# Key-index sums and the rotary of the latent heads on GpSimd instead of VectorE, in a two-block transformer kernel

## The chip, the cores and the metric

One core of a Trainium2 chip. The metric is the device time of one execution in microseconds (us), the median of several runs. All data is float32.

## What is computed

The reference runs a first block of two layers over 256 tokens of width 1024 and then a second block. Each of the two layers modulates and normalises x, projects it (`w_in`), runs four kinds of attention side by side (four heads of 64 each), projects back, and goes on to a feed-forward part (dense in layer 0, eight experts in layer 1). The four kinds are A (differential), B (latent), C (indexed sparse) and D (banded). The change touches two pieces of them:

```
# B, latent attention: rotary on the last 32 of each query head's 96 values and on the shared key part
q = concatenate([q[..., :64], apply_rope(q[..., 64:], cos, sin)])
k_rope = apply_rope(kr, cos, sin)
k = concatenate([k_nope, broadcast(k_rope)])
# apply_rope: [x1*cos - x2*sin, x1*sin + x2*cos], halves of 16

# C, indexed sparse attention: a score for each key, summed over eight index heads with weights
score = relu(einsum('bqhd,bsd->bqhs', qib, k_idx))
score = einsum('bqhs,bqh->bqs', score, wb)
score = where(mask, score, -inf)
top_val, top_idx = top_k(score, 64)
```

Only the 64 chosen keys take part in C's softmax.

## The kernel before, in words

The kernel is one program with a stream of instructions for each engine, written out by hand in order; semaphores are the only link between engines, and nothing is reordered. SyncE streams the weights in chunks of 1 MB into a ring of six; ScalarE and VectorE split each piece into a high and a low part (L1118 and L1688), and TensorE makes three products of each (L565 to L567). In the attention no weights are split, until its end.

The 256 tokens are two blocks of 128 rows (b = 0, 1) on the partitions. A unit of attention, such as A10, is a kind, a block b and a part; block 0 sees 128 keys, block 1 sees 256. For A the parts are the two terms of the difference, for I (the key index of C) they are index heads 0 to 3 and 4 to 7. A unit goes through:

- TensorE's `score` (L769): four heads into PSUM. TensorE waits for the result of the unit two places before.
- VectorE's `bias` (L1866 to L1869): scale and bias table added in PSUM, then the negative maximum of each head. Units I have none.
- ScalarE's `probabilities`: exponentials (L1292), or for I a ReLU (L1287), from PSUM into `PR`, a tile with two places (`place(...) % 2`) of four heads of up to 256 keys. Before it writes, ScalarE waits until the unit two places before has been used. For A10 that is I00's sum, for A11 I01's sum, for B00 I10's sum and for B10 I11's sum (semaphore `idx_added`); for I10 it is the turn of A11.
- TensorE's `turn` (L783) and ScalarE's `copy_pT` (L1302), TensorE's `values` (L798), VectorE's `store` (L1923).

The order of scores is A00 A01 I00 I01 A10 A11 I10 I11 B00 B10 D00 D10 C00 C10. VectorE's order is in its `attention`, printed below. There:

- `index_add` (L1883): `total = src * weight + total`, four instructions in a row for a unit's four heads, each waiting for the one before; the first takes the mask `cmask` (part 0) or the sum so far (part 1). The total lies in `picks[b]`. `w16` (weights) comes from `prepare_index` (semaphore `c_ready`).
- `select_keys` (L1894 to L1896): eight rounds of MAX8 and MATCH_REPLACE8 on the total, for block 0 after `combine` of A11, for block 1 after the store of B00.
- `rope_latent`: when ScalarE has copied B4 and B5, the up-projected keys and values (`copy_latent_out`, L1262), it makes the rotary of the four query heads and of the shared key part (L1952 to L1957) for both blocks, and copies the keys into `KB` (L1967, L1968). TensorE's fills B6 to B9 (L698) wait for it (`b_roped`), and ScalarE copies each out of PSUM (L1270). In TensorE's order: fill B6, fill B7, score I11, fill B8, turn A11, fill B9, fill D0, scores B00 and B10.
- `combine` (L1903 to L1909) makes the difference of A's two terms in place.
- `store_squares` and `store_normed` normalise A's output. Between them GpSimd raises four sums to the power -0.5 (`root`, L451; asked with L1623, taken with `take_root`).

In the attention GpSimd has one memset (`KI4`) and three such powers, in the order `root(0, 4)`, `root(4, 8)`, `root(4, 8)`. Outside it GpSimd issues the loads of the modulation weights `ada` (L438), each behind VectorE's use of an earlier one (`ada_used`), and some tables. SyncE's ring loads wait for VectorE's low parts of the weights.

## Time and profile before

| what | value |
|---|---|
| median of 3 runs | 2196.5 us (2195.31 to 2198.93) |
| the profiled execution's own time | 2199.03 us |
| its span, first to last instruction | 2197.3 us |
| mean granted TensorE clock | 0.963 |
| attention of layer 0 and of layer 1 (TensorE's first fill to its first product after it) | 120.5 to 201.4 us, 506.0 to 586.5 us |

How to read it: L12 is line 12 of the kernel. PE is TensorE's products, PEld its weight loads, DVE VectorE, ACT ScalarE, POOL GpSimd, SP SyncE. A timeline row has the start in us from the span's start, the duration in us (of all `xN` instructions together), engine, line, operation, output and inputs with partitions x elements, and in brackets the idle time of the engine ahead of it with what ended it. `arena` holds `PR` and the projections, `xt_words` the sums, `KB` and small tiles, `ps` is PSUM. Waits are inferred from semaphore events.

### The profile page before, as it was taken

The page shows a single profiled execution, that of the slowest core. Times are in us where ns is not written, and L with a number is a line of the kernel's source. Part 1 is how long each engine was busy: PE and PEld are TensorE (multiplying, and loading weights), DVE is VectorE, ACT ScalarE, POOL GpSimd, SP SyncE. Part 2 cuts the span into 40 slices and gives each one's busy share as a digit, 9 for nine tenths or more (in the row PEclk, how much of TensorE's full clock was granted, in tenths as well). Part 3 has the DMA queues.
Part 4 walks back from the last instruction along what each step waited for, and adds up shares of the span by engine and source line. Part 5 has one row for each costly group of instructions (what it writes and reads, how often), then busy time and mean ns, then how long its engine had stood idle before and what let it go on. Part 6 is the DMA issues. An engine that isn't in the chain of part 4 may idle for free.

```text
span 2197.3 us, 26426 instructions
## 1 busy us (share of the span) xinstructions
PE 2058.7 (94%) x9646; PEld 1699.0 (77%) x9646; DVE 1674.2 (76%) x2026; ACT 1333.9 (61%) x1834; POOL 55.6 (3%) x92
## 2 busy tenths in 40 slices
PE   3978999997899999999999999999979999889998
PEld 2757788885778888888888888888858887777887
DVE  5777677786668999989898999989986555345554
ACT  1444344444448878888887878888864445464443
POOL 1000000000000000000000000000000000000000
PEclk8987999998799999999999999999989999989999
DMA  8922587671159989999998989999965554304551
GB/s 348 367 103 88 195 333 295 262 300 50 60 231 351 375 336 374 362 347 363 347 368 345 373 338 373 363 347 364 374 233 195 188 192 153 134 20 156 190 191 58
DMA packets 80615, 573.67 MB, mean 261 GB/s; under 512 B 9088, under 2 KB 9728, under 8 KB 12272
## 3 DMA queue, kind: packets, MB, share of 16 engines
q1 hardware_dynamic: 70112, 508.59, 60.8%
q0 software_dynamic: 7936, 57.05, 6.7%
q10 hardware_dynamic: 2448, 6.41, 0.8%
q8 instruction: 78, 1.28, 0.2%
q14 instruction: 41, 0.34, 0.0%
HBM read 570.97 MB, written 1.05 MB: 260 GB/s over the span
## 4 chain that ended last, share of the span: by engine, by line
PE 85%; DVE 8%; ACT 3%; DMA 2%; issue 1%; POOL 1%; ACTq 0%; DVEq 0%; POOLq 0%
PE ps L565 25%; PE ps L567 25%; PE ps L566 25%; DMA Z<-in_ada 1%; PE ps L964 1%; PE ps L516 1%; PE ps L937 1%; PE ps L769 1%; PE ps L798 1%; DMA arena<-in_ada 1%; ACT arena L1292 1%; PE ps L783 1%; DVE Z L1593 1%; PE ps L629 1%; DVE xt_words L1895 1%
## 5 line engine op out<-in xcount | busy, mean ns | idle before, releaser
L2144 DVE TENSOR_TENSOR weights_low<-ring,weights_high 128x1024 fp32r<-128x1024 f32 x668 | 797.3, 1222 | 47.6 <-ACT weights_high L1396 34.9
L1396 ACT ACTIVATE weights_high<-ring 128x1024 fp32r<-128x1024 f32 x668 | 706.7, 1060 | 92.2 <-PE ps L567 79.2
L565 PE MATMUL ps<-weights_high,xt_high 128*128 128x512 f32 x1832 | 735.0, 401 | 13.1 <-DVE xt_low L1664 5.2
L567 PE MATMUL ps<-weights_high,xt_low 128*128 128x512 f32 x1832 | 719.1, 393 | 0.0
L566 PE MATMUL ps<-weights_low,xt_high 128*128 128x512 f32 x1832 | 718.6, 392 | 0.0
L1118 ACT ACTIVATE weights_high<-ring 128x1024 fp32r<-128x1024 f32 x298 | 313.7, 1058 | 309.7 <-PE ps L567 294.6
L1688 DVE TENSOR_TENSOR weights_low<-ring,weights_high 128x1024 fp32r<-128x1024 f32 x298 | 362.2, 1223 | 177.2 <-ACT weights_high L1118 176.8
L565 PEld LDWEIGHTS ps<-weights_high,xt_high 128*128 128x128 f32 x1832 | 346.8, 189 | 84.0 <-DVE xt_low L1664 5.7
L567 PEld LDWEIGHTS ps<-weights_high,xt_low 128*128 128x128 f32 x1832 | 346.4, 189 | 74.1
L566 PEld LDWEIGHTS ps<-weights_low,xt_high 128*128 128x128 f32 x1832 | 347.5, 190 | 68.4 <-issue 0.8
L565 PE MATMUL ps<-weights_high,hT_high 128*128 128x512 f32 x688 | 268.5, 390 | 1.2 <-DVE hT_low L2154 1.2
L567 PE MATMUL ps<-weights_high,hT_low 128*128 128x512 f32 x688 | 267.7, 389 | 0.0
L566 PE MATMUL ps<-weights_low,hT_high 128*128 128x512 f32 x688 | 267.7, 389 | 0.0
L565 PEld LDWEIGHTS ps<-weights_high,hT_high 128*128 128x128 f32 x688 | 129.1, 188 | 28.5 <-DVE hT_low L2154 1.6
L566 PEld LDWEIGHTS ps<-weights_low,hT_high 128*128 128x128 f32 x688 | 129.2, 188 | 26.9 <-issue 0.2
L567 PEld LDWEIGHTS ps<-weights_high,hT_low 128*128 128x128 f32 x688 | 129.1, 188 | 26.9
L1405 ACT ACTIVATE hT_high<-ps 128x256 fp32r<-128x256 f32 x112 | 42.8, 382 | 49.5 <-PE ps L937 49.5
L451 POOL TENSOR_TENSOR rstd<-rstd,minus_half 128x1 f32<-128x1 f32 (+2 forms) x28 | 22.7, 811 | 1754.9 <-DVE rstd L1623 1754.8
L516 PE MATMUL ps<-xt_words,X 128*128 128x128 f32 x160 | 26.6, 340 | 42.9 <-DVE xt_words L1639 42.8
L2154 DVE TENSOR_TENSOR hT_low<-ps,hT_high 128x256 fp32r<-128x256 f32 x112 | 46.8, 418 | 22.9 <-ACT hT_high L1405 22.9
L1401 ACT ACTIVATE FS<-ps 128x256 f32<-128x256 f32 x112 | 43.0, 384 | 30.8 <-PE ps L567 30.8
L798 PEld LDWEIGHTS ps<-arena 128*128 128x128 f32 x320 | 50.2, 244 | 12.3 <-issue 6.8
(234 smaller groups left out, 1444.7 us busy)
## 6 DMA issues: line engine op xcount, KB each, us to landing
ring<-in_stream SPq DMA_DIRECT2D x483, 1024.0 KB, 4.9
Z<-in_ada POOLq DMA_DIRECT2D x42, 1024.0 KB, 5.9
arena<-in_ada POOLq DMA_DIRECT2D x6, 1024.0 KB, 16.7
Z<-in_na POOLq DMA_DIRECT2D x1, 2048.0 KB, 7.8
Z<-in_dil POOLq DMA_DIRECT2D x1, 2048.0 KB, 13.5
band<-in_band ACTq DMA_DIRECT2D x2, 768.0 KB, 19.6
X<-in_x SPq DMA_DIRECT2D x1, 1024.0 KB, 11.3
gate_mix<-in_rows ACTq DMA_DIRECT2D x2, 512.0 KB, 8.9
```

The source lines that it names most:

```text
L516: return nc.tensor.matmul(ps[:, kt // 2, (kt % 2) * T + b * P:(kt % 2) * T + (b + 1) * P], source[:, b, kt * P:(kt + 1) * P], diag, start= ...
L565: nc.tensor.matmul(out, xh, wh, start=n, stop=False, skip_group_check=True)
L566: nc.tensor.matmul(out, xh, wl, start=False, stop=False, skip_group_check=True)
L567: return nc.tensor.matmul(out, xl, wh, start=False, stop=last, skip_group_check=True)
L798: m = nc.tensor.matmul(ps[:, 6, h * HD:(h + 1) * HD], PT[:, h, kb, :], PROJ[:, kb, c:c + HD], start=kb == 0, stop=kb == u.nk // P - 1)
L1118: act.activation(WH[:, p % SPLITS, :], ring[:, chunk % RING, half * PIECE:(half + 1) * PIECE], ACT.Copy).then_inc(hi_ready, 1)
L1396: act.activation(WH[:, slot, :], raw, ACT.Copy).then_inc(m["hi_ready"], 1)
L1401: act.activation(sgt[:, par, :], ps[:, 4 + par, 0:FW], ACT.Silu).then_inc(m["silu_ready"], 1)
L1405: act.activation(hTH[:, par].rearrange("p f n -> p (f n)"), ps[:, 6 + par, 0:2 * P], ACT.Copy).then_inc(m["hT_hi"], 1)
L1688: nc.vector.tensor_tensor(WL[:, p % SPLITS, :], ring[:, chunk % RING, half * PIECE:(half + 1) * PIECE], WH[:, p % SPLITS, :].bitcast(F32), ...
L2144: nc.vector.tensor_tensor(WL[:, slot, :], raw, WH[:, slot, :].bitcast(F32), ALU.subtract).then_inc(m["lo_ready"], 1)
L2154: nc.vector.tensor_tensor(hTL[:, par].rearrange("p f n -> p (f n)"), ps[:, 6 + par, 0:2 * P], hTH[:, par].rearrange("p f n -> p (f n)").bi ...
```

## The change

VectorE's `index_add`, `rope` and `rope_latent` go, and GpSimd gets them. The rotary keeps its instructions. The index sum has another form: one multiplication of all four heads by their weights, in place in `PR`, one addition of two heads to two, one of one to one, and one to the mask or to the sum so far: four instructions where each waits for the one before by a new semaphore, `pool_turn` (`turned_by`). The semaphores that others wait for (`idx_added`, `b_roped`) are unchanged. GpSimd's three powers stand in one list with the new work, `attention_sums`. VectorE's order is else unchanged.

```diff
+            turns = [0]
+            def index_add(layer, name):
+                u = UNIT[name]
+                b, nk, number = u.b, u.nk, INDEXED(layer, name)
+                total = picks[b][:, 0, :]
+                pool.wait_ge(probs, WEIGHED(layer, name))
+                if u.part == 1:
+                    pool.wait_ge(idx_added, number - 1)
+                rows = PR[:, place(layer, name) % 2, :, 0:nk]
+                weights = w16[:, b, 4 * u.part:4 * u.part + 4]
+                at = 0 if b == 0 else 128
+                heads = rows.rearrange("p (a b) k -> p a b k", a=2)
+                slots = weights.rearrange("p (b a) -> p a b", b=2).unsqueeze(3).broadcast_to([P, 2, 2, nk])
+                turned_by(pool.tensor_tensor(heads, heads, slots, ALU.mult))
+                turned_by(pool.tensor_tensor(rows[:, 0:2, :], rows[:, 0:2, :], rows[:, 2:4, :], ALU.add))
+                turned_by(pool.tensor_tensor(rows[:, 0, :], rows[:, 0, :], rows[:, 1, :], ALU.add))
+                ins = pool.tensor_tensor(total, rows[:, 0, :], cmask[:, at:at + nk] if u.part == 0 else total, ALU.add)
+                ins.then_inc(idx_added, 1)
+            def rope(x, b):
...
+                pool.tensor_tensor(TR[:, 0, 0:n], x1, cos, ALU.mult)
+                pool.tensor_tensor(TR[:, 1, 0:n], x2, sin, ALU.mult)
+                pool.tensor_tensor(TR[:, 2, 0:n], x1, sin, ALU.mult)
+                turned_by(pool.tensor_tensor(TR[:, 3, 0:n], x2, cos, ALU.mult))
+                pool.tensor_tensor(x1, TR[:, 0, 0:n], TR[:, 1, 0:n], ALU.subtract)
+                turned_by(pool.tensor_tensor(x2, TR[:, 2, 0:n], TR[:, 3, 0:n], ALU.add))
+            def turned_by(ins):
+                turns[0] += 1
+                ins.then_inc(pool_turn, 1)
+                pool.wait_ge(pool_turn, turns[0])
+            def rope_latent(layer):
+                pool.wait_ge(filled, FILLED(layer, "B5"))
+                for b in range(NB):
+                    q = PROJ[:, b, B_UQ:B_UQ + 384].rearrange("p (h n) -> p h n", h=4)
+                    rope(q[:, :, 64:96], b)
+                    rope(PROJ[:, b, B_KR:B_KR + 32].unsqueeze(1), b)
+                    kv = PROJ[:, b, B_UKV:B_UKV + 512].rearrange("p (h n) -> p h n", h=4)
+                    pool.tensor_copy(KB[:, b, :, 0:64], kv[:, :, 0:64])
+                    ins = pool.tensor_copy(KB[:, b, :, 64:96],
+                                           PROJ[:, b, B_KR:B_KR + 32].unsqueeze(1).broadcast_to([P, 4, 32]))
+                ins.then_inc(b_roped, 1)
+            def attention_sums(layer):
+                root(0, 4)
+                pool.wait_ge(c_ready, layer + 1)
+                index_add(layer, "I00")
+                index_add(layer, "I01")
+                root(4, 8)
+                rope_latent(layer)
+                index_add(layer, "I10")
+                index_add(layer, "I11")
+                root(4, 8)
...
-            root(0, 4)
-            for b in range(NB):
-                root(4, 8)
+            attention_sums(0)
...
-            root(0, 4)
-            for b in range(NB):
-                root(4, 8)
+            attention_sums(1)
...
                 combine(layer, 0)
-                index_add(layer, "I00")
-                index_add(layer, "I01")
                 bias(layer, "A10")
                 store_squares(layer, "A01")
                 bias(layer, "A11")
-                rope_latent(layer)
                 combine(layer, 1)
                 select_keys(layer, 0)
-                index_add(layer, "I10")
                 store_normed(layer, "A01")
-                index_add(layer, "I11")
                 bias(layer, "B00")
```

## Rows read from the trace of the kernel before

**Rows 1.** The page's first part: busy time of each engine.

```profile
PE 2058.7 (94%) x9646; PEld 1699.0 (77%) x9646; DVE 1674.2 (76%) x2026; ACT 1333.9 (61%) x1834; POOL 55.6 (3%) x92
```

**Rows 2.** Windows view, two stretches of the first attention.

```profile
core 0: us, PE busy (x) PEld busy (x) DVE busy (x) ACT busy (x) POOL busy (x), PEclk, DMA share, GB/s
139.00:162.00 23.00, 15.91 (x84) 11.64 (x83) 21.66 (x78) 11.52 (x28) 1.01 (x1) 0.93 0.00 1
162.00:190.00 28.00, 22.32 (x133) 19.07 (x132) 24.78 (x54) 12.04 (x46) 1.01 (x1) 0.73 0.00 1
```

**Rows 3.** The chain that ended last: start us, us, what.

```profile
159.45 0.48 DVE xt_words L1883
...
168.59 2.09 PE ps L769 x8
...
170.71 1.24 DVE ps L1866
```

**Rows 4.** VectorE's timeline, first attention: start us, us, instruction, idle before.

```profile
136.43 2.74 DVE L1883 SCALAR_TENSOR_TENSOR xt_words<-arena,w,xt_words 128x128 f32<-128x128 f32 x7
...
145.54 0.21 DVE L1952 TENSOR_TENSOR xt_words<-arena,cossin 128x64 f32<-128x64 f32 x1
...
149.71 0.22 DVE L1968 COPY xt_words<-arena 128x128 f32<-128x128 f32 x1
...
158.41 1.53 DVE L1883 SCALAR_TENSOR_TENSOR xt_words<-arena,w,xt_words 128x256 f32<-128x256 f32 x3
...
160.65 2.04 DVE L1883 SCALAR_TENSOR_TENSOR xt_words<-arena,w,xt_words 128x256 f32<-128x256 f32 x4
```

**Rows 5.** Timeline of all engines, first attention, ahead of the rotary.

```profile
128.21 0.23 DVE L1623 TENSOR_SCALAR rstd<-ss 128x2 f32<-128x2 f32 x2
...
136.99 1.13 PE L769 MATMUL ps<-arena 32*128 32x256 f32 x8
...
141.89 0.47 ACT L1292 ACTIVATE arena<-ps,nmax 128x256 f32<-128x256 f32 x1
...
143.69 0.62 ACT L1262 ACTIVATE arena<-ps 128x512 f32<-128x512 f32 x1
```

**Rows 6.** GpSimd's timeline, up to the loads after the first attention.

```profile
5.71 0.12 POOL L461 MEMSET minus_half<- 128x8 f32 x1
...
117.69 0.95 POOL L470 MEMSET FS<- 128x1024 f32 x1 [0.34 <-DVE lamc L2284]
...
128.52 1.04 POOL L451 TENSOR_TENSOR rstd<-rstd,minus_half 128x4 f32<-128x4 f32 x1 [9.88 <-DVE rstd L1623]
...
213.35 0.59 POOL L438 DMA_DIRECT2D Z<-in_ada  x1 [44.19 <-DVE Z L1593]
```

**Rows 7.** Timeline of two powers on GpSimd beside VectorE.

```profile
433.41 1.22 DVE L1688 TENSOR_TENSOR weights_low<-ring,weights_high 128x1024 fp32r<-128x1024 f32 x1
...
433.57 1.46 POOL L451 TENSOR_TENSOR rstd<-rstd,minus_half 128x1 f32<-128x1 f32 x1 [2.13 <-DVE rstd L1623]
...
1834.04 1.21 DVE L1764 SCALAR_TENSOR_TENSOR arena<-ps,band 128x1024 f32<-128x1024 f32 x1
...
1834.20 0.56 POOL L451 TENSOR_TENSOR rstd<-rstd,minus_half 128x1 f32<-128x1 f32 x1 [2.15 <-DVE rstd L1623]
```

**Rows 8.** Timeline of all engines after the rotary, first and second attention.

```profile
156.61 1.02 ACT L1287 ACTIVATE arena<-ps 128x1024 f32<-128x1024 f32 x1 [3.58 <-PE ps L783]
...
159.34 1.01 ACT L1287 ACTIVATE arena<-ps 128x1024 f32<-128x1024 f32 x1
...
159.99 2.79 PE L769 MATMUL ps<-arena 96*128 96x128 f32 x16
...
166.51 0.47 ACT L1292 ACTIVATE arena<-ps,nmax 128x256 f32<-128x256 f32 x1 [0.41 <-DVE nmax L1869]
...
528.83 0.62 ACT L1262 ACTIVATE arena<-ps 128x512 f32<-128x512 f32 x1
...
551.66 0.47 ACT L1292 ACTIVATE arena<-ps,nmax 128x256 f32<-128x256 f32 x1 [0.41 <-DVE nmax L1869]
```

More of the change, by code:

```diff
@@ L345, in program @@
         fill_ps, filled = sem("fill_ps"), sem("filled")
+        pool_turn = sem("pool_turn")
         ki_cleared = sem("ki_cleared")
@@ new lines, in rope @@
+            def rope(x, b):
+                n = x.shape[1]
+                cos = cossin[:, b, 0, :].unsqueeze(1).broadcast_to([P, n, 16])
+                sin = cossin[:, b, 1, :].unsqueeze(1).broadcast_to([P, n, 16])
+                x1, x2 = x[:, :, 0:16], x[:, :, 16:32]
+                pool.tensor_tensor(TR[:, 0, 0:n], x1, cos, ALU.mult)
[4 more added lines that the diff above has]
+                turned_by(pool.tensor_tensor(x2, TR[:, 2, 0:n], TR[:, 3, 0:n], ALU.add))
@@ L1869, in bias @@
                 nc.vector.tensor_reduce(nmax[:, par, :], src, AX_X, ALU.max, negate=True).then_inc(biased, 1)
-            def index_add(layer, name):
-                u = UNIT[name]
-                b, nk, number = u.b, u.nk, INDEXED(layer, name)
-                total = picks[b][:, 0, :]
-                dve.wait_ge(probs, WEIGHED(layer, name))
-                if u.part == 1:
-                    dve.wait_ge(idx_added, number - 1)
-                for h in range(4):
-                    src = PR[:, place(layer, name) % 2, head_slot(h), 0:nk]
-                    at = 0 if b == 0 else 128
-                    prev = cmask[:, at:at + nk] if u.part == 0 and h == 0 else total
-                    ins = nc.vector.scalar_tensor_tensor(total, src, w16[:, b, 4 * u.part + h:4 * u.part + h + 1], prev,
-                                                         ALU.mult, ALU.add)
-                    if h < 3:
-                        link(ins)
-                ins.then_inc(idx_added, 1)
             def select_keys(layer, b):
@@ L1944, in store_normed @@
                                         ALU.mult).then_inc(mixed, 1)
-            def rope(x, b):
-                n = x.shape[1]
-                cos = cossin[:, b, 0, :].unsqueeze(1).broadcast_to([P, n, 16])
-                sin = cossin[:, b, 1, :].unsqueeze(1).broadcast_to([P, n, 16])
-                x1, x2 = x[:, :, 0:16], x[:, :, 16:32]
-                nc.vector.tensor_tensor(TR[:, 0, 0:n], x1, cos, ALU.mult)
-                nc.vector.tensor_tensor(TR[:, 1, 0:n], x2, sin, ALU.mult)
-                nc.vector.tensor_tensor(TR[:, 2, 0:n], x1, sin, ALU.mult)
-                link(nc.vector.tensor_tensor(TR[:, 3, 0:n], x2, cos, ALU.mult))
-                nc.vector.tensor_tensor(x1, TR[:, 0, 0:n], TR[:, 1, 0:n], ALU.subtract)
-                link(nc.vector.tensor_tensor(x2, TR[:, 2, 0:n], TR[:, 3, 0:n], ALU.add))
-            def rope_latent(layer):
-                dve.wait_ge(filled, FILLED(layer, "B5"))
-                for b in range(NB):
-                    q = PROJ[:, b, B_UQ:B_UQ + 384].rearrange("p (h n) -> p h n", h=4)
-                    rope(q[:, :, 64:96], b)
-                    rope(PROJ[:, b, B_KR:B_KR + 32].unsqueeze(1), b)
-                    kv = PROJ[:, b, B_UKV:B_UKV + 512].rearrange("p (h n) -> p h n", h=4)
-                    nc.vector.tensor_copy(KB[:, b, :, 0:64], kv[:, :, 0:64])
-                    ins = nc.vector.tensor_copy(KB[:, b, :, 64:96],
-                                                PROJ[:, b, B_KR:B_KR + 32].unsqueeze(1).broadcast_to([P, 4, 32]))
-                ins.then_inc(b_roped, 1)
             def norm_latent(layer):
```

## The prediction

> **What bounds the kernel now.** First the page's totals [rows 1]: TensorE is busy 94% of the span and GpSimd 3%. This is an average over stages, and the change touches only two of them, the attention of the two layers, some 80 us each of 2197.3. The windows view [rows 2] shows the first one apart. From 139 to 162 us VectorE is busy 21.66 of 23.00 us, TensorE 15.91; from 162 to 190 VectorE has 24.78 of 28.00. The reader is to see that VectorE carries the middle of the attention. The chain that ended last [rows 3] says the same: it runs through VectorE's index sums (L1883, at 159.45), and later through TensorE's scores of D10 at 168.59 and VectorE's bias of D10 at 170.71. So the work to be moved lies on the path that sets the end, and its time is a candidate gain. How much is gained depends on what ends second, and on how fast GpSimd does the work.
>
> **What is removed.** In layer 0 VectorE does I00 and I01 in eight instructions (seven take 2.74 us: 3.1), the rotary and the copies from 145.54 to 149.93 (4.4), I10 in four (three take 1.53: 2.0) and I11 in 2.04 [rows 4]: 11.5 us a layer, 23 in the two. That would be the gain if nothing else ended later. It can't be all: ScalarE's copy of B5 ends at 143.69 + 0.62 = 144.31 [rows 5], at the end of a row of TensorE and ScalarE steps (B2, B3, B4, the exponentials of A10, B5) that waits neither for an index sum nor for a late step of VectorE. That part stays where it is.
>
> **What is added: the price on GpSimd.** The trace has no multiplication or addition on GpSimd, so I bound it. Fixed part of an instruction: the powers of 128x1 and 128x4 take 0.56 and 1.04 us [rows 6, 7], 0.16 for each element and 0.40 beside it; a memset of 128x8 takes 0.12 and reads nothing. So 0.10 is the lower end and 0.40 the upper; the power's own preparation is in the latter, so I take half of it, 0.20. Part of an element: a memset of 1024 elements takes 0.95 us [rows 6], 0.93 ns each for writing alone, the lower end. Two operands and a result, one after another, would be 2.8 ns, the upper end. I take 1.9: the operands read in turn, the result beside them. A wait on a semaphore: VectorE's request ends at 128.44 and the power starts at 128.52 [rows 5, 6]; 0.1 us each.
> - I00, I01: four instructions of 512, 256, 128, 128 elements: 1024 x 1.9 ns + 4 x 0.2 + 3 waits x 0.1 = 3.05 us each (VectorE 1.55).
> - I10, I11: 2048 elements: 3.9 + 0.8 + 0.3 = 5.0 us each (VectorE 2.0); ends 2.6 and 7.6.
> - Rotary: 24 two-input instructions of 64 or 16 elements (960 in all, 1.8 us), four copies (768 elements at 0.93 ns, 0.7), 28 x 0.2 = 5.6, eight waits 0.8: 8.9 us (VectorE 4.4); ends 5.2 and 15.4.
> GpSimd gets 25 us more a layer. Its total says that it has room; what counts is when each result is wanted. Between the memset at 117.69 and the next ada load at 213.35 it issues no DMA [rows 6], so none is held up behind the new work, and SyncE's ring loads wait for VectorE's low parts of weights, which come after it.
>
> **One interference.** Two powers of 128x1 took 0.56 and 1.46 us [rows 7]. The short one ran beside a VectorE instruction that reads PSUM and one SBUF tile (L1764), the long one beside one with two SBUF inputs (L1688, 1.22 us), and ended 0.4 us after it. So a VectorE instruction with two SBUF inputs holds GpSimd up. Here that is combine of A11 (L1909, four instructions of 256 elements, 2.0 us at L1883's rate of I10), which will fall into the rotary. I add 0.3 us a layer, and 2.0 at most. The Trainium skill (SBUF — State Buffer, "Who interferes with whom") says that whichever of the two engines starts first holds a shared port pair for the whole instruction; the trace agrees for GpSimd as the loser (1.46 against 0.56), and no row shows VectorE as the loser. By that rule GpSimd's long multiplications would also hold up VectorE's squares of A11, which have slack; the sum would be the same.
>
> **The sum, layer 0.** (1) I00 runs from 136.0 to 139.1, I01 to 142.2; ScalarE's exponentials of A10 (141.89) wait for I00 and don't feel it. (2) VectorE biases A10 when its scores end (136.99 + 1.13) and asks for the root of A01 at 142.3; GpSimd answers by 143.5. (3) The rotary needs B5 (144.31); GpSimd starts it at 144.4, 1.1 us before VectorE did, and ends it at 153.3 instead of 149.93: **3.4 us late**. (4) From there the order written out for TensorE and ScalarE follows at fixed distance: fills B6 and B7, scores of I11, fill B8, the turn of A11, ScalarE's result of I10 (157.63 before), of I11 (160.35) [rows 8]. VectorE's earlier combine doesn't help, since the fills stand ahead of that turn. So I10's data is there at 161.0. (5) GpSimd finishes I10 at 166.0 and I11 at 171.0, without a gap, for I11's data comes only 2.7 us after I10's. (6) The exponentials of B10 overwrite I11's place and wait for that sum: they start at 171.1 instead of 166.51 [rows 8], 4.6 late. VectorE's side is earlier: the scores of B00 and B10 end by 162.78 + 3.4, the bias of B10 at 168.7. (7) Behind the exponentials come the scores of D10 and VectorE's bias of D10, at 175.3 instead of 170.71. The root for A11 is queued on GpSimd behind I11: answered at 172.1, A11 stored by 173.0. This new wait is covered by 2.3 us; without cover it would cost its 1.0. (8) From the bias of D10 on nothing is removed. VectorE selects keys, then biases C00 and C10 in the same order, so the delay runs on to the end of the layer.
> As a formula: delay = rotary + 2 x I1x - 14.3 us, with 14.3 = 166.51 - 144.4 - 7.7 - 0.1 (7.7 is 157.63 - 149.93). 8.9 + 10.0 makes 4.6; with the interference 4.9. Layer 1 has the same distances: from B5's copy to B10's exponentials 551.66 - 528.83 = 22.83 us, against 22.82 in layer 0 [rows 5, 8]. So it counts twice: **+9.8 us**. VectorE's idle time grows by 16 us a layer and buys nothing. The profiled execution took 2199.03 us for a span of 2197.3, and would take 2208.8. The median of the three runs is 2.5 us lower, so I predict 2196.5 + 9.8 = 2206.3.
> The Trainium skill (GPSIMD Engine Reference, "Performance versus the Vector engine") gives 4497 ns for a GpSimd addition of 2048 elements and advises VectorE for elementwise work, a rule against this change; no row here shows it. An estimate by that page, 2.2 ns an element beside my fixed part, would make the delay 6.4 us a layer.
>
> **Rivals.**
> - GpSimd is nearer its upper ends. At 0.3 us fixed and 2.3 ns the rotary is 12.1 us and I1x 6.2: delay 10.2 a layer, 2217. At the ends, 15.4 + 15.2 + 2.0 - 14.3 = 18.3 a layer, 2233. For it: the power's 0.40 is of the same kind of instruction. Against it: the power's loop is no addition. 16%.
> - GpSimd is near its lower fixed price (0.10): rotary 6.1, I1x 4.6, delay 1.0 a layer, 2198.5, which is no measurable change (within 0.2%, 4.4 us, about what a measurement of this kernel can tell from none). For it: the memsets. 18%.
> - **The other side: VectorE's path shortens.** Place: the bias of B10, for which the exponentials waited (166.51). If GpSimd finished I11 before that bias, only the fills would count, and the bias would be done at 144.4 + rotary + 15.3 (162.78 - 149.93, and 2.45 for the bias). This decides from rotary + 2 x I1x below 14.3. At the lower ends (5.2, 2.6) it is done at 164.9 against 166.4: 1.5 us a layer, 2193.5; with VectorE's own rotary of 4.4, 2.3 a layer, 2191.9, the only part beyond 0.2%. For it: VectorE does carry the stage [rows 2]. Against it: I1x's first instruction alone reads 1024 elements of each operand. 6%.
> - The change doesn't do what it says: nothing in it keeps these instructions from GpSimd, and none touches PSUM; under 1%.
>
> **How the numbers follow.** My forecast (2203 to 2212) has 60%, the slow rival 16%, no change 18%, the faster one 6%. The range, 2198 to 2219, leaves out the last, a part of the third and the far upper ends. Slower by over 0.2% is the forecast and nearly all of the slow rival, 0.75; faster 0.04; the rest, 0.21, within it.
>
> **What would show it.** In the changed profile: GpSimd some 50 us busier; the rotary starting at 144.4 and lasting 8 to 10 us; ScalarE's exponentials of B10 waiting for GpSimd instead of VectorE's maximum; the bias of D10 some 5 us later; VectorE idle before the biases of B00 and D10. A rotary under 6 us with I1x under 4.5 would make the prediction wrong, as would any shorter distance after the bias of D10.

## The result, and the profile after

The changed kernel takes 2200.2 us (median of 20 runs, 2195.2 to 2209.04) and the kernel before beside it 2194.88 us (20 runs). The ratio is 1.0031, 95% interval 1.0022 to 1.0041, or +6.8 us on 2196. The forecast was +9.8, slower, with 2198 to 2219 as its range. The single times of the changed kernel fall in two groups, 11 at 2195.2 to 2200.7 us and 9 at 2203.0 to 2209.0, and the trace read below (2199.59 us) is of the lower one. Here and below, a difference in us with a ratio beside it is that ratio taken on 2196 us; it needn't equal the difference of the medians printed (5.3 here). Four single executions of 3002 to 5374 us (one of before_again, one of held_before, two of the kernel before beside them) are left out of the ratios.

The first part of the page of the changed kernel:

```profile
PE 2053.2 (93%) x9646; PEld 1694.5 (77%) x9646; DVE 1654.9 (75%) x1938; ACT 1334.5 (61%) x1834; POOL 100.9 (5%) x180
```

GpSimd has 45 us more than in [rows 1]. VectorE has 19 less. The forecast's 23 were counted from first start to last end, with the gaps between small instructions, and a few of VectorE's other instructions take longer beside GpSimd (the squares of A01, at 142.47, 0.63 us instead of 0.42). The windows view of the same two stretches as in [rows 2]:

```profile
139.00:162.00 23.00, 14.76 (x68) 9.99 (x64) 15.08 (x42) 7.58 (x23) 12.67 (x36) 0.85 0.00 1
162.00:190.00 28.00, 22.44 (x127) 19.79 (x127) 20.02 (x47) 13.59 (x43) 10.33 (x9) 0.70 0.00 1
```

VectorE's 21.66 and 24.78 have become 15.08 and 20.02, and nothing ended sooner for it. GpSimd's timeline in the first attention, which has no counterpart before:

```profile
137.39 1.04 POOL L469 TENSOR_TENSOR arena<-arena,w 128x512 f32<-128x512 f32 x1 [7.05 <-ACT arena L1349]
138.51 0.73 POOL L470 TENSOR_TENSOR arena<-arena 128x256 f32<-128x256 f32 x1
139.31 0.46 POOL L471 TENSOR_TENSOR arena<-arena 128x128 f32<-128x128 f32 x1
...
143.84 1.02 POOL L452 TENSOR_TENSOR rstd<-rstd,minus_half 128x4 f32<-128x4 f32 x1 [0.42 <-DVE rstd L1685]
145.62 0.32 POOL L481 TENSOR_TENSOR xt_words<-arena,cossin 128x64 f32<-128x64 f32 x1 [0.76 <-ACT arena L1324]
...
147.53 0.22 POOL L481 TENSOR_TENSOR xt_words<-arena,cossin 128x16 f32<-128x16 f32 x1
...
149.43 0.51 POOL L481 TENSOR_TENSOR xt_words<-arena,cossin 128x64 f32<-128x64 f32 x1
...
153.70 0.29 POOL L503 COPY xt_words<-arena 128x128 f32<-128x128 f32 x1
...
162.53 1.89 POOL L469 TENSOR_TENSOR arena<-arena,w 128x1024 f32<-128x1024 f32 x1 [8.54 <-ACT arena L1349]
164.51 1.26 POOL L470 TENSOR_TENSOR arena<-arena 128x512 f32<-128x512 f32 x1
...
167.52 1.89 POOL L469 TENSOR_TENSOR arena<-arena,w 128x1024 f32<-128x1024 f32 x1
...
171.79 0.72 POOL L472 TENSOR_TENSOR xt_words<-arena,xt_words 128x256 f32<-128x256 f32 x1
```

The rotary runs from 145.62 to 153.99, 8.4 us; I10 and I11 from 162.53 to 172.51, 5.0 us each and back to back. The timeline of ScalarE and VectorE at the end of that row, against 166.51 and 170.71 in [rows 3, 8]:

```profile
165.90 0.70 DVE L1928 SCALAR_TENSOR_TENSOR ps<-ps,cmask 128x512 f32<-128x512 f32 x1 [7.98 <-PE ps L831]
...
172.54 0.47 ACT L1354 ACTIVATE arena<-ps,nmax 128x256 f32<-128x256 f32 x1 [3.13 <-POOL xt_words L472]
...
173.51 0.43 DVE L1986 TENSOR_TENSOR XN<-XN,rstd 128x256 f32<-128x256 f32 x1 [0.40 <-POOL rstd L452]
...
176.74 1.23 DVE L1928 SCALAR_TENSOR_TENSOR ps<-ps,band 128x1024 f32<-128x1024 f32 x1 [2.34 <-PE ps L831]
```

The exponentials of B10 start at 172.54 and wait for GpSimd's last sum. VectorE stands idle 7.98 us ahead of the bias of B00 and 2.34 ahead of that of D10. Then a part of the delay is given back in this execution. TensorE's timeline at the end of the attention, before:

```profile
198.05 3.68 PE L798 MATMUL ps<-arena 128*128 128x64 f32 x16 [0.26 <-ACT arena L1302]
201.48 0.77 PE L565 MATMUL ps<-weights_high,xt_high 128*128 128x512 f32 x1
202.06 0.63 PE L566 MATMUL ps<-weights_low,xt_high 128*128 128x512 f32 x1
```

and after:

```profile
204.10 2.00 PE L860 MATMUL ps<-arena 128*128 128x64 f32 x16 [0.26 <-ACT arena L1364]
205.91 0.48 PE L627 MATMUL ps<-weights_high,xt_high 128*128 128x512 f32 x1
206.22 0.39 PE L628 MATMUL ps<-weights_low,xt_high 128*128 128x512 f32 x1
```

The same 16 products take 2.00 us instead of 3.68, and a product of 128x512 0.39 instead of 0.63: in this execution TensorE has its full clock (2.4 GHz) here, where before it had half (1.2 GHz).

**Marks.** The text below compares kernels by five marks, in us after VectorE's bias of A00 (125.09 before, 125.87 after; the first attention / the second). Front means up to the bias of D10. The first product is the first of the output projection (L565, L627 in the changed kernel), some 30 us behind the bias of D10. The gate is TensorE's product for the gate modulation (L688 before, L750 after). All from timelines, one execution each.

| kernel | rotary ends | exps of B10 | bias of D10 | first product | gate | D10 to gate |
|---|---|---|---|---|---|---|
| before | 24.84 / 25.62 | 41.42 / 42.21 | 45.62 / 46.25 | 76.39 / 77.03 | 91.67 / 90.83 | 46.05 / 44.58 |
| before_again | 25.92 / 25.56 | 43.33 / 42.14 | 47.25 / 46.24 | 76.15 / 77.02 | 89.44 / 90.74 | 42.19 / 44.50 |
| after | 28.12 / 27.74 | 46.67 / 46.08 | 50.87 / 50.27 | 80.04 / 79.17 | 93.34 / 92.98 | 42.47 / 42.71 |
| as_changed | 28.14 / 28.58 | 46.71 / 47.23 | 50.90 / 51.43 | 80.39 / 80.91 | 95.85 / 94.60 | 44.95 / 43.17 |
| sums_only | 24.87 / 24.63 | 43.83 / 42.58 | 48.03 / 46.78 | 77.39 / 76.15 | 90.69 / 87.65 | 42.66 / 40.87 |
| rotary_only | 27.97 / 27.59 | 45.22 / 44.62 | 49.30 / 48.82 | 80.08 / 79.60 | 95.65 / 93.20 | 46.35 / 44.38 |
| early_sums | 24.85 / 25.08 | 42.35 / 41.67 | 46.17 / 45.86 | 74.94 / 74.27 | 88.24 / 87.87 | 42.07 / 42.01 |
| three_sums | 25.00 / 25.03 | 41.79 / 41.23 | 45.39 / 45.43 | 74.59 / 74.00 | 90.22 / 87.65 | 44.83 / 42.22 |
| split_rotary | 24.03 / 24.25 | 39.66 / 39.88 | 43.85 / 44.07 | 74.63 / 73.50 | 90.07 / 84.97 | 46.22 / 40.90 |
| padded | 31.28 / 31.47 | 50.34 / 49.98 | 54.53 / 54.17 | 83.92 / 83.33 | 97.22 / 94.79 | 42.69 / 40.62 |
| held_before | 25.42 / 25.72 | 42.00 / 42.31 | 45.60 / 45.92 | 74.13 / 74.64 | 87.43 / 86.15 | 41.83 / 40.23 |
| held_changed | 28.11 / 28.53 | 46.66 / 47.16 | 49.91 / 50.41 | 75.74 / 77.57 | 89.06 / 89.06 | 39.15 / 38.65 |
| held_split | 24.03 / 23.37 | 39.67 / 39.01 | 43.27 / 42.62 | 70.44 / 68.45 | 83.76 / 79.95 | 40.49 / 37.33 |
| filled_before | 25.42 / 25.78 | 42.00 / 42.37 | 45.60 / 45.98 | 73.94 / 74.31 | 89.39 / 87.92 | 43.79 / 41.94 |

### The profile page after: what moved, and what is told of

Same layout as the page of the kernel before. It is cut to its first block, busy times and chain, and to the rows that moved or that the text cites. A ratio compares the mean times of both kernels' runs of the same rounds, so it can differ in the third digit from the quotient of the medians.

```text
span 2197.6 us, 26428 instructions
## 1 busy us (share of the span) xinstructions
PE 2053.2 (93%) x9646; PEld 1694.5 (77%) x9646; DVE 1654.9 (75%) x1938; ACT 1334.5 (61%) x1834; POOL 100.9 (5%) x180
## 4 chain that ended last, share of the span: by engine, by line
PE 86%; DVE 5%; ACT 3%; POOL 2%; DMA 2%; issue 1%; ACTq 0%; DVEq 0%; POOLq 0%
PE ps L627 25%; PE ps L629 25%; PE ps L628 25%; PE ps L831 2%; PE ps L860 1%; PE ps L845 1%; PE ps L1026 1%; PE ps L999 1%; ACT arena L1354 1%; DMA Z<-in_ada 1%; DMA arena<-in_ada 1%; PE ps L578 1%; PE ps L760 1%; DVE weights_low L1750 1%; DVE Z L1655 1%
## 5 line engine op out<-in xcount | busy, mean ns | idle before, releaser
L627 PE MATMUL ps<-weights_high,xt_high 128*128 128x512 f32 x1832 | 732.9, 400 | 14.3 <-DVE xt_low L1726 5.2
L627 PEld LDWEIGHTS ps<-weights_high,xt_high 128*128 128x128 f32 x1832 | 345.7, 189 | 85.0 <-DVE xt_low L1726 5.7
L627 PE MATMUL ps<-weights_high,hT_high 128*128 128x512 f32 x688 | 268.4, 390 | 1.2 <-DVE hT_low L2167 1.2
L627 PEld LDWEIGHTS ps<-weights_high,hT_high 128*128 128x128 f32 x688 | 129.1, 188 | 28.5 <-DVE hT_low L2167 1.6
L1239 ACT ACTIVATE FS<-ps 128x512 f32<-128x512 f32 x33 | 19.8, 599 | 63.9 <-PE ps L629 63.9
## 6 DMA issues: line engine op xcount, KB each, us to landing
Z<-in_dil POOLq DMA_DIRECT2D x1, 2048.0 KB, 13.3
```

The source lines that it names most:

```text
L627: nc.tensor.matmul(out, xh, wh, start=n, stop=False, skip_group_check=True)
```

## The experiments

Three accounts were set against each other. **G**: the late rotary and GpSimd's queue set the exponentials of B10, and the delay runs on. **S**: VectorE and GpSimd hold each other up when both work on SBUF ("shared access" in the expectations). **C**: what a delay is worth in the end is decided by where TensorE's low clock falls behind the bias of D10.

### The change taken apart

**as_changed** is the changed kernel itself, for a second trace and time of it.

> The changed kernel as it is, beside the others on one chip. Account G (GpSimd's queue sets the start of B10's exponentials: rotary 8.4 us, then two sums of 5.0 us; part of the delay comes back where TensorE's granted clock is higher at the out-projection): delay of the bias of D10 against the attention's start 5.2 us in each layer, as in the first trace; the time 2 to 10 us above before, and a wider spread of single times than before. Account S (shared access: what is lost is lost to VectorE and GpSimd holding each other up): the same delay, but the GpSimd rows beside VectorE's combine carry it. Account C (the clock alone: more low-clock time in the attention): the delay of D10's bias would differ between two traces of this kernel by as much as the low-clock time does.

Measured: 2206.06 us (12 runs) against 2196.69 (30 runs), ratio 1.0032 (1.0015 to 1.005), +7.0 us (the medians differ by 9.4). Again there are two groups, 4 runs at 2196.5 to 2199.2 and 8 at 2204.9 to 2208.6; the profiled one (2206.93) is of the upper. Its trace has the front of the first one to 0.04 us in the first attention, but takes 44.95 us from D10 to the gate instead of 42.47. In the second attention its bias of D10 is 1.16 us later than the first trace's.

**sums_only**: the sums stay on GpSimd, the rotary goes back.

```diff
 root(4, 8)
-rope_latent(layer)
 index_add(layer, "I10")
...
 bias(layer, "A11")
+rope_latent(layer)
 combine(layer, 1)
```

The first line taken out is GpSimd's, the one put in VectorE's, with the `rope` of before.

> All four index sums on GpSimd, the rotary back on VectorE. Account G: the rotary ends at 149.8 as before (bias of A11 ends at 145.4 and VectorE needs 4.4), I10's data is there 7.7 later, GpSimd needs 2 x 5.0, so B10's exponentials start about 1.1 us later than before in each layer, and the time is 1 to 3 us above before. Account S: no GpSimd instruction meets combine here, so the kernel would be as fast as before or faster. Account that the sums are what costs most: 3 us or more a layer remain, 2201 or more.

Measured: 2191.77 us, ratio 0.9975 (0.9957 to 0.9992), -5.5 us: **faster**, against account G, which had 1 to 3 us above; S had allowed "as fast as before or faster". Its front is late, as G has it (2.41 and 0.37 us at the exponentials of B10, 1.1 expected). From the timelines of ScalarE and VectorE in this kernel:

```profile
169.26 0.47 ACT L1353 ACTIVATE arena<-ps,nmax 128x256 f32<-128x256 f32 x1 [3.12 <-POOL xt_words L472]
...
173.46 1.23 DVE L1927 SCALAR_TENSOR_TENSOR ps<-ps,band 128x1024 f32<-128x1024 f32 x1 [2.34 <-PE ps L830]
```

The exponentials of B10 still wait for GpSimd, and the bias of D10 is 2.41 and 0.53 us late, yet the gate is 0.98 and 3.18 us early. The gain lies behind D10.

**rotary_only**: the reverse.

```diff
 pool.wait_ge(c_ready, layer + 1)
-index_add(layer, "I00")
-index_add(layer, "I01")
 root(4, 8)
 rope_latent(layer)
-index_add(layer, "I10")
-index_add(layer, "I11")
 root(4, 8)
```

All four sums are VectorE's again, with the code and the places of before.

> The rotary on GpSimd, all index sums back on VectorE. Account G: the rotary ends about 3.3 us later than before, I10's and I11's data come 3.3 to 4.1 us later, VectorE adds them when they come and only then biases B00 and B10, so B10's exponentials start 2.6 to 3.3 us later in each layer: 2200 to 2202, less what the clock gives back. Account that the sums cost most: within 1 us of before. Account S: the four multiplications beside combine (0.50 instead of 0.32 us) alone are late, 0.7 us a layer, 2196.

Measured: 2200.96 us, ratio 1.0011 (1.0002 to 1.0021), +2.4 us (the medians differ by 4.3). The rotary alone makes the bias of D10 3.68 and 2.57 us late.

**three_sums**: as sums_only, with I10 back on VectorE as well, so that only I11 follows on GpSimd.

```diff
 index_add(layer, "I01")
 root(4, 8)
-index_add(layer, "I10")
 index_add(layer, "I11")
...
 select_keys(layer, 0)
+index_add(layer, "I10")
```

> I00, I01 and I11 on GpSimd, I10 and the rotary on VectorE. Account G: I10 is done by VectorE at 159.7 as before, GpSimd adds I11 from 160.4 to 165.4 while VectorE biases B00 and B10 (until 165.3), so B10's exponentials start about 1 us earlier than before in each layer: 1 to 2 us below before. Accounts by which any work on GpSimd costs (its sums being slower, or shared access): at or above before.

Measured: 2192.53 us, ratio 0.9972 (0.9961 to 0.9984), -6.1 us, faster than both kernels and than the 1 to 2 us below that G had. The exponentials of B10 are back about where they were before (+0.37 and -0.98 us) and wait for VectorE's maximum again: with the rotary on VectorE and one long sum on GpSimd the late end of the queue is gone. S, which had this kernel at or above before, doesn't explain it.

### The slope: less, more, and before once more

**early_sums**: only I00 and I01 on GpSimd (I10, I11 and the rotary on VectorE). The edit is shown against sums_only; VectorE gets its own two sums back.

```diff
 index_add(layer, "I01")
 root(4, 8)
-index_add(layer, "I10")
-index_add(layer, "I11")
 root(4, 8)
```

> Only I00 and I01 on GpSimd; I10, I11 and the rotary on VectorE as before. Account G: these two sums end long before anything waits for GpSimd, and VectorE's work from the rotary on is that of before, so the bias of D10 stands within 0.5 us of before's 45.62 and 46.25 and the time within 1.5 us of before. Account S: VectorE is held up beside GpSimd's sums, +1 to +3 us. Account C, by which two and three sums off VectorE help only through where the low clock falls: the bias of D10 as before, and the gate modulation 1 to 3 us a layer earlier, 2 to 5 us in all.

Measured: 2192.87 us, ratio 0.9986 (0.9977 to 0.9995), -3.1 us, with the bias of D10 in its place (+0.55 and -0.39) and the gate 3.43 and 2.96 us earlier. That is about C's forecast (the gate 1 to 3 us earlier in each layer, 2 to 5 us in all); G alone had the time within 1.5 us of before, which the interval just reaches (1.1), and S had it above before.

**split_rotary**: three_sums, with block 0 of the rotary on VectorE and block 1 on GpSimd.

```diff
-for b in range(NB):
+for b in (1,):
...
+for b in (0,):
...
-pe.wait_ge(b_roped, layer + 1)
+pe.wait_ge(b_roped, 2 * (layer + 1))
```

The first loop is that of GpSimd's `rope_latent`, which gets small tiles of its own, the second that of VectorE's.

> Three sums on GpSimd (I00, I01, I11), I10 on VectorE, and the rotary divided: block 0 on VectorE, block 1 on GpSimd at the same time. Account G (the end of the rotary and GpSimd's queue set the front): the rotary ends about 1 to 2 us earlier after the attention's first bias than before's 24.84 and 25.62, the data of I10 and the exponentials of B10 come as much earlier, the bias of D10 stands 43.5 to 45 us after the start (before 45.62 and 46.25), and the time is 2 to 5 us below three_sums' 2192.5. Account S (the two engines hold each other up): the two halves run beside each other and take longer than their shares, the rotary ends no earlier than before's, and the time is that of three_sums or more. Account C (TensorE's clock alone decides what an earlier front is worth): the front is earlier, but the first product of the output projection isn't, and the time stays within 2 us of three_sums.

Measured: 2187.38 us, ratio 0.9959 (0.9943 to 0.9975), -9.0 us. The rotary ends 0.81 and 1.37 us before that of the kernel before, the bias of D10 stands 1.77 and 2.18 us ahead. Account S shows here as well. From the timeline of both engines in this kernel:

```profile
158.89 0.42 DVE L2004 TENSOR_TENSOR XN<-XN,rstd 128x256 f32<-128x256 f32 x1
159.12 1.94 POOL L470 TENSOR_TENSOR arena<-arena,w 128x1024 f32<-128x1024 f32 x1 [9.59 <-DVE xt_words L1945]
159.34 2.00 DVE L2005 TENSOR_TENSOR XN<-XN,gdiff 128x256 f32<-128x256 f32 x1
161.14 1.33 POOL L471 TENSOR_TENSOR arena<-arena 128x512 f32<-128x512 f32 x1
161.26 0.69 DVE L1928 SCALAR_TENSOR_TENSOR ps<-ps,cmask 128x512 f32<-128x512 f32 x1
```

VectorE's multiplication of 128x256 from two SBUF tiles takes 0.42 us alone (the changed kernel has it at 173.97 with 0.42) and 2.00 here: it starts 0.22 us behind GpSimd's long one and ends only when that has ended. That costs VectorE 1.6 us ahead of the bias of B00, and the kernel is still the faster one. The second attention shows the same 2.00, at 542.30.

**padded**: the changed kernel with the added line four times for each block on GpSimd.

```diff
 kv = PROJ[:, b, B_UKV:B_UKV + 512].rearrange("p (h n) -> p h n", h=4)
+turned_by(pool.tensor_copy(KB[:, b, :, 0:64], kv[:, :, 0:64]))
 pool.tensor_copy(KB[:, b, :, 0:64], kv[:, :, 0:64])
```

> The changed kernel with four more copies of a block's keys (0.39 us each, and a wait behind each) ahead of the block's last copies on GpSimd: the rotary ends some 3.6 us later in each layer. Account G with the delay running to the end: the bias of D10 3.6 us later than as_changed's 50.90 and 51.43 in each layer and the time 7.2 us above as_changed. Account C: the front as by G, but TensorE's clock gives back a share behind the bias of D10, so the time is 2 to 6 us above. If the time rises by less than 1 us, the rotary isn't on the path that sets the end.

Measured: 2204.56 us, ratio 1.0050 (1.0031 to 1.0069), +11.0 us, or 4.0 above as_changed by the ratios (each of the two is known to about 4 us). C had 2 to 6, G with the whole delay 7.2. The rotary ends 3.14 and 2.89 us later than in as_changed and the bias of D10 3.63 and 2.74, 6.4 in the two.

**before_again**: the kernel before, no edit.

> The kernel before, unchanged, for a second trace of it. If the marks up to the bias of D10 agree with the first trace's within 0.5 us and those behind it, with the place of the low clock, don't, then the distance behind D10 belongs to an execution and not to a kernel (account C). If all marks agree within 0.5 us, the shorter distances of the kernels with sums on GpSimd belong to the kernels. Time 2196.7 within 2 us.

Measured: 2196.74 us, ratio 1.0004 (0.9995 to 1.0013). The windows view from the bias of D10 to the gate, both attentions (window and its length, then busy us and instructions of PE, PEld, DVE, ACT and POOL, PEclk, DMA share, GB/s), first of before:

```profile
170.71:216.76 46.05, 40.36 (x189) 34.48 (x189) 33.28 (x60) 21.05 (x50) 0.59 (x1) 0.69 0.23 78
555.70:600.28 44.58, 40.71 (x188) 35.05 (x189) 29.58 (x56) 19.98 (x49) 0.00 (x0) 0.68 0.16 58
```

then of before_again:

```profile
172.77:214.96 42.19, 36.40 (x188) 31.15 (x188) 33.28 (x60) 21.07 (x50) 0.59 (x1) 0.78 0.24 84
555.45:599.95 44.50, 40.57 (x188) 34.93 (x189) 29.59 (x56) 20.00 (x49) 0.00 (x0) 0.68 0.16 58
```

In the second attention, at the same granted clock (0.68), the two executions agree within 0.1 us. In the first the clock is 0.78 instead of 0.69, and the same program needs 3.9 us less; VectorE's and ScalarE's busy times agree within 0.02 us. So the distance behind D10 is no constant of the kernel. The front isn't quite one either: the bias of D10 is 1.6 us later here.

### Holding the clock

The windows view of before, from just behind the bias of D10 on:

```profile
175.00:180.00 5.00, 3.55 (x32) 3.09 (x32) 4.63 (x16) 4.52 (x19) 0.00 (x0) 1.00 0.01 2
180.00:185.00 5.00, 3.11 (x17) 2.77 (x17) 4.71 (x13) 0.34 (x1) 0.00 (x0) 0.69 0.01 3
185.00:190.00 5.00, 5.00 (x25) 4.18 (x22) 3.41 (x4) 2.07 (x9) 0.00 (x0) 0.50 0.00 0
```

From 175 to 180 TensorE is busy 3.55 of 5 us at its full clock, in pieces between waits. In the next row the clock falls to half, and from 185 on it is half (0.50) while TensorE is busy throughout. These kernels fill the waits with products of 128x512 that nobody reads, by a helper that the kernel has already (`keep_busy(count, bank)`).

```diff
+keep_busy(5, 4)
 score(layer, "D00")
 turn(layer, "B00")
+keep_busy(4, 7)
...
 score(layer, "C00")
+keep_busy(4, 7)
 turn(layer, "D10")
+keep_busy(7, 7)
```

**held_before** has them in the kernel before.

> The kernel before with 20 products of 128x512 (bf16, nobody reads them) a layer on TensorE, put where it waits around the scores of D00, D10 and C00 and the turn of D10, about 4.3 us of work in gaps of 1.1 to 1.9 us each. Account C (behind the bias of D10 the distance is TensorE's clock): the granted clock of the 30 us from the bias of D10 on rises from 0.60 to 0.69 towards 1.00, the first product of the output projection comes 28.5 us or less behind the bias of D10 (before 30.8 and 30.8), the gate modulation comes 39 to 41 us behind it (before 46.05 and 44.58), and the time falls by 4 to 10 us. Against it: the work is not idle filling but delay, the clock stays as it was, and the time rises by 2 to 8 us.

Measured: 2188.53 us, ratio 0.9963 (0.9951 to 0.9975), -8.1 us. Its windows from D10 to the gate:

```profile
170.38:212.21 41.83, 36.41 (x199) 29.88 (x200) 33.30 (x61) 21.07 (x50) 0.59 (x1) 0.84 0.25 85
552.89:593.12 40.23, 36.25 (x198) 30.18 (x200) 29.59 (x57) 20.01 (x49) 0.00 (x0) 0.83 0.18 65
```

Work that nobody needs makes the kernel faster, with its front in place (45.60 and 45.92).

**held_changed** has them in the changed kernel.

> The changed kernel with the same 20 products at the same places. Account C: behind the bias of D10 the distance is as in held_before, so the whole of the front's delay shows: its time is 9 to 11 us above held_before's (the forecast's +9.8), where as_changed was 9.4 and the first measurement of the change 5.3 above before. Account G with a fixed share given back by something other than the clock: only 5 to 7 us above held_before. If the clock of that stretch doesn't rise, nothing is told by it.

Measured: 2191.85 us, ratio 0.9979 (0.9965 to 0.9992), -4.6 us. That is 3.5 above held_before by the ratios, not 9 to 11, nor the 5 to 7 of the rival: a miss of account C as it was put. Its windows:

```profile
175.49:214.64 39.15, 30.26 (x199) 24.60 (x200) 33.29 (x60) 21.17 (x50) 0.64 (x1) 1.00 0.26 88
557.68:596.33 38.65, 33.00 (x198) 27.37 (x200) 29.56 (x56) 20.12 (x49) 0.00 (x0) 0.91 0.19 68
```

The condition "the same clock in both" wasn't met: 1.00 and 0.91 here, 0.84 and 0.83 in held_before. The fronts differ by 4.31 and 4.49 us, the distances behind them by 2.68 and 1.58 the other way.

**held_split** has them in split_rotary.

> The split rotary with the same 20 products. Its bias of D10 stands 1.8 to 2.2 us a layer ahead of before's; with a clock held behind it, account C has the time 3.5 to 4.5 us below held_before's and below split_rotary's 2187.4. If the products only cost time, it is above 2187.4.

Measured: 2178.64 us (2178.2 to 2179.54), ratio 0.9923 (0.9908 to 0.9938), **-16.9 us**, the best version here. It is 8.8 below held_before by the ratios, where C had 3.5 to 4.5: its fronts are 2.3 and 3.3 us ahead of held_before's, and its distances behind D10 are shorter too. Its windows:

```profile
168.39:208.88 40.49, 33.28 (x199) 27.30 (x200) 33.30 (x61) 21.20 (x50) 0.64 (x1) 0.92 0.25 86
544.66:581.99 37.33, 30.20 (x199) 24.88 (x201) 29.55 (x57) 20.15 (x49) 0.00 (x0) 1.00 0.19 70
```

**filled_before** has 28 such products a layer in the kernel before, to bring its clock to 1.00 as well.

```diff
-keep_busy(4, 7)
+keep_busy(5, 7)
 turn(layer, "D10")
-keep_busy(7, 7)
+keep_busy(14, 7)
```

> The kernel before with 28 idle products a layer: as in held_before, with seven more behind the turn of D10, in the wait of 1.75 us that was left ahead of the low clock there. Account C: the clock stays at 1.00 from the bias of D10 to the gate modulation, as it did in layer 0 of held_changed; the distance between the two is then 38.7 to 39.2 us, that of held_changed's layer 0 (held_before had 41.83 and 40.23), the time is 2184.5 to 2187, and with the clock alike the gate modulation of held_changed's layer 0 (89.06) stands behind this one's by what its bias of D10 does, 4 to 4.5 us: the delay at the bias of D10 then reaches the gate whole. Against it: the clock is alike, the distance here is shorter or longer than 39 by over 1 us, and something else than the clock decides it; or the low clock stays at 13.7 us a layer and the time is held_before's 2188.5 or more, which leaves it open.

Measured: 2183.74 us, ratio 0.9953 (0.9937 to 0.997), -10.3 us. Its six executions fall in two groups: four at 2181.4 to 2185.0 us with a mean granted clock of 0.974 to 0.976 over the whole span, two at 2191.6 and 2191.7 with 0.970 and 0.971. The one that was profiled is of the second group:

```profile
170.26:214.05 43.79, 38.14 (x206) 30.70 (x208) 33.31 (x61) 21.15 (x50) 0.59 (x1) 0.84 0.24 81
552.67:594.61 41.94, 38.06 (x207) 30.93 (x209) 29.56 (x57) 20.10 (x49) 0.00 (x0) 0.84 0.18 63
```

So no trace has before's order with a clock of 1.00 behind the bias of D10, and the comparison that was wanted wasn't made. What the row shows is that the place counts too: at 0.84 in both, this execution needs 1.96 us more than held_before's. Here the low clock covers the first products of the output projection (the first 0.6 us each), there it ended ahead of them.

## Why the prediction was right or wrong

**(1), (2) the early sums and the root: right.** I00 and I01 take 2.92 and 2.97 us (3.05 forecast), and the root of A01 is answered at 144.86, later than forecast (143.5) but before the rotary can start.

**(3) the rotary: right.** It waits for B5's copy as forecast, takes 8.4 us (8.9) and ends 3.28 us late (3.4); in the second attention 2.12, in as_changed 2.96. An instruction of 64 elements takes 0.32 us and one of 16 takes 0.22, as priced. The interference is there: four instructions beside the combine of A11 take 0.49 to 0.51 us, 0.7 us more in all than alone, where 0.3 was added and 2.0 was the most. Without it the rotary would be 1.2 us shorter than priced, for an independent instruction starts 0.04 us before the last one ends.

**(4) a fixed distance to I10's data: off by 0.8.** It is 8.46 us, not 7.7. The windows view of exactly that stretch, before:

```profile
149.93:157.63 7.70, 5.90 (x28) 4.79 (x28) 7.08 (x31) 2.21 (x4) 0.00 (x0) 0.78 0.00 1
```

and after:

```profile
153.99:162.45 8.46, 6.66 (x28) 5.23 (x28) 3.59 (x15) 2.21 (x4) 0.00 (x1) 0.66 0.01 2
```

TensorE's 28 products take 6.66 us instead of 5.90, at a granted clock of 0.66 instead of 0.78; ScalarE's four take the same. This is the assumption of (8), a distance that doesn't change, failing in small.

**(5) the late sums: right.** 5.0 us each, without a gap. A multiplication by the weights costs 1.66 ns an element beside 0.19 us fixed (1.04 for 512, 1.89 for 1024), an addition 2.1 beside 0.19 (0.46, 0.73, 1.26 for 128, 256, 512). Thus I1x came out at 5.0 with its parts off on both sides of the 1.9 ns taken for all. The Trainium skill (GPSIMD Engine Reference, "Performance versus the Vector engine") gives 4497 ns for an addition of 2048 elements. No instruction here is that long; the additions of 128 to 512 elements agree with it if their line is drawn on, an estimate of 2048 x 2.1 ns + 0.19 us = 4.5 us. The multiplication here is cheaper, with 1.89 us for 1024 elements.

**(6), (7) the exponentials of B10 and the bias of D10: right.** +5.25 us at the exponentials in the first attention (4.9 forecast), the same at the bias of D10, and the new wait for the root of A11 is covered by 2.34 us (2.3). In the second attention it is 3.87 and 4.02, in as_changed 5.02 and 5.18. That 5.25 stands so near 4.9 is in part luck: a rotary 0.8 us shorter than priced with its interference, against 0.8 more in (4) and a start of the rotary 0.4 later behind the bias of A00. rotary_only and sums_only show that either move alone delays the bias of D10, by 3.68 and 2.41 us in the first attention and by 2.57 and 0.53 in the second; they don't add up to as_changed's 5.28 and 5.18, and the formula, in which both share one allowance of 14.3 us, doesn't ask them to.

**(8) failed**, as it was put: "From the bias of D10 on nothing is removed", "so the delay runs on to the end of the layer". The fronts of as_changed lose 10.5 us in the two layers, those of after 9.3, and +7.0 and +6.8 arrive. So the step that was mis-sized is the distance behind the front, put at no change: it gave back 2.5 to 3.4 us. That the time lay in the range all the same is owed to a range with room below. The text had named this as what would make it wrong, a shorter distance after D10. Of the ways in which that distance could change, it had none: it took it for a constant of the order of instructions. held_before and before_again show that it goes with TensorE's clock: in the first attention it is 46.05, 42.19 and 41.83 us at clocks of 0.69, 0.78 and 0.84, with the same instructions in the first two and some filling products more in the third.

All versions with work moved and no products added, side by side. Front is the change of the bias of D10 in both layers together, D10 to gate that of the distance behind it, rest all other changes up to the last instruction, and profiled their sum, the change of the profiled execution's span: all against the first trace of before. End is the ratio on 2196 us, over all executions.

| | front | D10 to gate | rest | profiled | end | end - front |
|---|---|---|---|---|---|---|
| before_again | +1.6 | -3.9 | +0.6 | -1.7 | +0.9 | -0.7 |
| split_rotary | -4.0 | -3.5 | -1.7 | -9.2 | -9.0 | -5.1 |
| three_sums | -1.1 | -3.6 | -1.5 | -6.1 | -6.1 | -5.1 |
| early_sums | +0.2 | -6.6 | +0.3 | -6.1 | -3.1 | -3.2 |
| sums_only | +2.9 | -7.1 | -1.8 | -6.0 | -5.5 | -8.4 |
| rotary_only | +6.3 | +0.1 | +0.7 | +7.0 | +2.4 | -3.8 |
| after | +9.3 | -5.5 | -3.6 | +0.3 | +6.8 | -2.5 |
| as_changed | +10.5 | -2.5 | -0.3 | +7.6 | +7.0 | -3.4 |
| padded | +16.8 | -7.3 | -9.5 | 0.0 | +11.0 | -5.9 |

A straight line of end against front through the eight rows of changed versions (after and as_changed are one kernel) has a slope of 1.03 and lies 4.8 us below zero at no delay. Among the changed versions, then, a delay of the front does run on nearly whole on average, as (8) says; between any of them and the kernel before there are 2.5 to 8.4 us which (8) doesn't have. The line is rough: its fronts are of one execution each, which spread by 1.6 us in before, and with the medians instead of the ratios it has 0.92 and 3.8.

Within one execution the sums close, and they show where a delay goes. In rotary_only's, the slowest of its 12, nothing is given back. In padded's, the fastest of its six, 16.8 us are given back whole, over half of it outside the stretch that the marks watch: from the gate of the second layer to the end it has 1587.86 us, before has 1597.02, after 1592.24 and as_changed 1596.89. A part of that lies right behind the gate:

```profile
600.28:620.28 20.00, 20.00 (x84) 15.24 (x83) 9.24 (x16) 3.18 (x3) 0.00 (x0) 0.83 0.23 83
609.44:629.44 20.00, 19.40 (x100) 15.21 (x99) 12.41 (x24) 4.41 (x6) 0.00 (x0) 1.00 0.29 104
```

The first row is of before, the second of padded, both 20 us long from the gate on: at full clock TensorE gets 100 products of the same sequence done instead of 84. The same places part the two traces of the changed kernel, 7.3 us apart in all: 1.2 at the fronts, 2.9 between D10 and gate, 3.2 elsewhere.

**How the clock sets the distance.** In the 28 attentions of the 14 traces the two parts of the distance from D10 to the gate take few values. From the first product to the gate the first attention takes 13.3 us in the eight traces in which its granted clock is 1.00, and 15.3 to 15.6 in the other six, at 0.84 to 0.86; the second takes 11.5 at 1.00, and 13.6 to 13.8 at 0.82 or 0.83. From the bias of D10 to the first product it is 25.83 us in the only two at full clock, the first attention of held_changed and the second of held_split:

```profile
175.49:201.32 25.83, 18.59 (x146) 15.29 (x148) 21.46 (x47) 15.44 (x45) 0.00 (x0) 1.00 0.01 2
544.66:570.49 25.83, 18.70 (x147) 15.40 (x148) 20.85 (x48) 15.47 (x45) 0.00 (x0) 1.00 0.00 1
```

Their biases of D10 stand 7.3 us apart (49.91 and 42.62), and the distance is the same. It is 30.77 or 30.78 in all six attentions with a clock of 0.61, of before, before_again, rotary_only and split_rotary; in all six the low clock runs from 11 to 12 us behind the bias of D10 to beyond the first product, and the biases of D10 stand at 43.85 to 49.30. So where the low clock falls in the same place behind D10, (8) holds to the first product: a delay is passed on whole. Its mean alone doesn't give the distance: four attentions at 0.62, with the low clock elsewhere, take 28.4 to 29.2 us. The first attentions of before and of after:

```profile
170.71:201.48 30.77, 26.74 (x136) 23.68 (x137) 22.02 (x48) 16.31 (x45) 0.00 (x0) 0.61 0.00 1
176.74:205.91 29.17, 28.22 (x137) 25.12 (x137) 21.46 (x47) 15.44 (x45) 0.00 (x0) 0.53 0.00 1
```

After has the lower clock and is 1.6 us shorter. TensorE waits 4.0 us in before's stretch and only 0.95 in after's, and before has the low clock at its end, where TensorE is busy throughout and its timeline above shows 3.68 us for the products that take after 2.00. The place of the low clock counts, as account C said. Why it falls in another place when work leaves VectorE stays open, and so does how often each place occurs over many executions: one trace of a kernel shows one.

**The rivals.** "GpSimd is slow" and "low fixed price" fall by the measured 8.4 us for the rotary and 5.0 for a late sum. The other side, a shorter path on VectorE, didn't happen in the change, but three_sums and split_rotary are it: with the rotary kept or divided, the exponentials of B10 no longer wait long or at all for GpSimd, and the front is earlier than before.

## What to carry to other kernels

Moving work from a full engine to an idle one pays where the idle engine's result isn't wanted next. Here the early sums and one late sum left the front about in its place, and the rotary and a second long sum in a row did not; half the rotary on either engine beat both kernels. A distance read from one trace is a constant only as far as the clock in it is: read PEclk over the stretch behind a change, and take a second trace of the kernel before, ahead of adding the delay to the end. Add up the changes within one execution before comparing them with averages over many. And where TensorE runs at half clock behind a row of short waits, try to fill them: 20 products a layer that nobody reads took 8 us off the kernel before and as much off the split one.

## What the runs showed of the hardware

- VectorE as the loser: an instruction of 0.42 us with two SBUF inputs took 2.00 us when it started 0.22 us behind a GpSimd multiplication of 1.94. The Trainium skill (SBUF — State Buffer, "Who interferes with whom") says that a VectorE instruction with two SBUF inputs contends with a GpSimd instruction that reads SBUF, and that the order in which they are issued decides which of them is blocked. The trace agrees, in both attentions of split_rotary; the trace of before had shown only the other direction (1.46 against 0.56 in [rows 7]).
- Small two-input instructions of the two engines run beside each other at a smaller price: in split_rotary VectorE's of 64 elements take 0.21 to 0.35 us, GpSimd's 0.32 to 0.34.
- The spread of single times goes with the clock: before ran from 2184.69 to 2202.55 us in 30 runs, at mean granted clocks of 0.971 to 0.960 over the span; held_split, at 0.976 and 0.977 in all six, from 2178.2 to 2179.54. The mean doesn't tell all of it: the changed kernel's two groups lie at 0.962 to 0.967 and 0.961 to 0.965.
